# First pairs of the second attention: query evictions on two engines, squares in pieces, another order of products

## The reference

```
q = _rms_norm((hn @ p['w_b_q'][j]).reshape(b, l, B_HEADS, B_HD), p['g_b_qn'][j])   # 16 heads of 64
c_k = jnp.cumsum(logf_all, axis=1)                                                  # forget gates
s = q . k * (d ** -0.5) + (c_q - c_k);  s = where(mask, s, -inf)
p = softmax(s, axis=-1);  o = p . v
h = h + o.reshape(b, l, B_HEADS * B_HD) @ p['w_b_out'][j]
```

## Time and profile before

| | |
|---|---|
| median of 3 runs (lowest to highest) | 2285.42 us (2283.72 to 2291.73) |
| the profiled execution, its own time | 2283.86 us |
| its span, first to last instruction | 2281.5 us |
| mean granted clock of TensorE | 0.987 |
| first scores of pair 0 begin | 1676.78 us from the span's start |
| first transposes of pair 0 / second head's transposes | 1685.74 / 1698.30 us |
| pair 0 ends, pair 1 ends, pair 2 ends | 1714.27 / 1737.24 / 1757.15 us |

### The profile page before, as it was taken

The page is one execution under the profiler, slowest core; times in us unless marked ns, Lnnn a source line. Parts: engine busy times, 40 slices in busy tenths (PEclk is TensorE's granted clock), DMA queues, the critical chain, the costliest instruction groups (busy, mean ns, idle before and its releaser), DMA issues.

```text
span 2281.5 us, 45750 instructions
## 1 busy us (share of the span) xinstructions
PE 2226.9 (98%) x16695; PEld 2147.8 (94%) x16695; DVE 1687.2 (74%) x2718; ACT 1084.9 (48%) x1832; POOL 308.4 (14%) x276
## 2 busy tenths in 40 slices
PE   8999999999999999999999999999989999999998
PEld 8999999988889999999978999999878899999998
DVE  7984984478886896697446995896367868966983
ACT  6542543456765652354324551453257755533541
POOL 0000002035552000000123000001134520000001
PEclk9999999999999999999999999999999999999999
DMA  3222232100002222222223322223212222232222
GB/s 115 92 100 94 93 116 93 46 26 21 15 19 74 84 101 90 89 108 100 73 86 111 112 99 95 93 92 121 74 48 48 50 75 81 95 105 87 93 100 78
DMA packets 73903, 187.58 MB, mean 82 GB/s; under 512 B 40853, under 2 KB 44389, under 8 KB 62537
## 3 DMA queue, kind: packets, MB, share of 16 engines
q1 hardware_dynamic: 72520, 181.73, 23.5%
q0 software_dynamic: 1280, 4.49, 0.6%
HBM read 178.75 MB, written 7.35 MB: 82 GB/s over the span
## 4 chain that ended last, share of the span: by engine, by line
PE 89%; DVE 6%; ACT 2%; issue 2%; DVEq 0%; POOL 0%; DMA 0%; ACTq 0%; SPq 0%
PE ps L731 21%; PE ps L665 19%; PE ps L667 18%; PE ps L666 18%; PE ps L834 6%; PE ps L1104 1%; PE ps L929 1%; PE ps L1040 1%; PE ps L683 1%; DVE hid_lo L2045 1%; PE ps L1131 1%; DVE arena L2499 0%; DVE x_lo L2045 0%; DVE stat L2402 0%; DVE w_lo L2035 0%
## 5 line engine op out<-in xcount | busy, mean ns | idle before, releaser
L665 PE MATMUL ps<-xs_hi,w_hi 128*128 128x272 f32 x1408 | 409.4, 291 | 1.1 <-DVE scratch L2153 1.1
L667 PE MATMUL ps<-xs_hi,w_lo 128*128 128x272 f32 x1408 | 407.9, 290 | 0.0
L666 PE MATMUL ps<-xs_lo,w_hi 128*128 128x272 f32 x1408 | 407.1, 289 | 0.0
L1402 ACT ACTIVATE w_hi<-raw 128x1408 fp32r<-128x1408 f32 (+4 forms) x123 | 146.1, 1188 | 456.8 <-PE ps L731 223.9
L1463 ACT ACTIVATE w_hi<-w_blocks 128x1024 fp32r<-128x1024 f32 x176 | 186.9, 1062 | 308.8 <-PE ps L667 157.8
L666 PE MATMUL ps<-xs_lo,w_hi_more 128*128 128x272 f32 x1056 | 306.6, 290 | 0.0
L665 PE MATMUL ps<-xs_hi,w_hi_more 128*128 128x272 f32 x1056 | 306.5, 290 | 0.0
L665 PEld LDWEIGHTS ps<-xs_hi,w_hi 128*128 128x128 f32 x1408 | 266.2, 189 | 2.3 <-issue 1.3
L731 PE MATMUL ps<-hid_hi,w_hi 128*128 128x256 f32 (+1 forms) x1290 | 265.7, 287 | 1.3 <-DVE w_lo L2035 1.0
L667 PEld LDWEIGHTS ps<-xs_hi,w_lo 128*128 128x128 f32 x1408 | 266.9, 190 | 0.0
L666 PEld LDWEIGHTS ps<-xs_lo,w_hi 128*128 128x128 f32 x1408 | 266.3, 189 | 0.0
(11 more groups left out here) (307 smaller groups left out, 5051.3 us busy)
## 6 DMA issues: line engine op xcount, KB each, us to landing
w_blocks<-w_ffn_in SPq DMA_DIRECT2D x88, 1024.0 KB, 4.8
raw<-w_ffn_out SPq DMA_DIRECT2D x64, 704.0 KB, 4.1
raw<-w_b_kv SPq DMA_DIRECT2D x16, 512.0 KB, 3.2
raw<-w_a_out SPq DMA_DIRECT2D x8, 512.0 KB, 3.3
raw<-w_b_q SPq DMA_DIRECT2D x8, 512.0 KB, 3.3
raw<-w_b_out SPq DMA_DIRECT2D x8, 512.0 KB, 3.3
raw<-w_a_in SPq DMA_DIRECT2D x4, 672.0 KB, 3.9
raw<-w_a_qup SPq DMA_DIRECT2D x8, 288.0 KB, 2.9
```

The costliest lines, as they stand in the source:

```text
L665: pe.matmul(out, lhs[0], rhs[0], start=start, stop=False, skip_group_check=more)
L666: pe.matmul(out, lhs[0], rhs[1], start=False, stop=False, skip_group_check=more)
L667: return pe.matmul(out, lhs[1], rhs[0], start=False, stop=stop, skip_group_check=more)
L1402: act.activation(wh[par][:, 0:n], raw[par][:, 0:n], ACT.Copy).then_inc(w_hi, 1)
```

## The change

1. Taking the second chunk: tiles 0, 1, 2 go to ScalarE (`take_query`), between its first exponentials; tiles 3 and 4 stay with VectorE and come after the reciprocals of the first head. `inverse_sum(0, 4, 0)` moves behind `top(1, 0, 0)`.
2. TensorE no longer waits for c0 and c4 ahead of pair 0. Inside pair 0 it waits for c1, c2 (ScalarE's) and c4 where the banks are first written. Of the 22 `keep_clock` matmuls 4 stay, ahead of `turn(0, 0, 0)`.
3. Squares and sums of the second chunk are made tile by tile: ScalarE squares tile 0, 1, 2, 3 and 4 at four places of pair 0, VectorE sums tiles 0, 1, 2 at three places of pair 0 and tiles 3, 4 at the end of pair 1, where it also makes the means.
4. A tiny exponential (`load_exp`) is issued on ScalarE ahead of `low_rows`.
5. In every staged pair the products `values(0, p)` j = 1, 2, 3 stand together; the wait for the bank of `ts` is ahead of j = 3, not of j = 1, and the transposes `ts` come after all of them.
6. Pair 1 is written out too; the loops cover pairs 2 to 6.

```diff
 TOKQ = {"act": ["sq", "sq4"], "dve": ["c0", "c1", "c2", "c3", "c4", "ss", "ss4", "ms"]}
+TOKQ1 = {"act": ["c0", "c1", "c2"] + [f"sq{t}" for t in range(5)],
+         "dve": ["c3", "c4"] + [f"ss{t}" for t in range(5)] + ["ms"]}
...
     def pair_b(p, stages):
         uses, before = w_uses(L, p, True, stages, False, mla), w_uses(L, p - 1, True, True, stages, mla)
+        first = isinstance(p, int) and p == 0
         scores(1, 0, p)
+        if first:
+            pe.wait_ge(*Q["k"][1]["act"].at("c1"))
+            keep_clock(7, 4, xa[0])
         turn(0, 0, p, uses, before)
+        if first:
+            pe.wait_ge(*Q["k"][1]["act"].at("c2"))
         turn(0, 1, p, uses, before)
         scores(1, 1, p)
+        if first:
+            pe.wait_ge(*Q["k"][1]["dve"].at("c4"))
         turn(0, 2, p, uses, before)
         scores(1, 2, p)
-        if isinstance(p, int) and p == 0:
-            keep_clock(7, 10, xa[0])
         scores(1, 3, p)
...
-        values(0, p, range(1, 2), (lambda: bank_of("ts", uses, before)) if stages else None)
+        values(0, p, range(1, 4), (lambda: bank_of("ts", uses, before)) if stages else None)
         if stages:
             staged_samples(p + 1, uses)
-        values(0, p, range(2, 4))
         if not stages:
             first_tile(XO, range(2))
         turn(1, 0, p, uses, before, not stages)
...
         for u in range(5):
-            if u == 3:
-                pe.wait_ge(*Q["k"][1]["dve"].at("c0"))
-            if u > 2:
-                keep_clock(7, 6, xa[0])
             scores(0, u, 0)
-        pe.wait_ge(*Q["k"][1]["dve"].at("c4"))
         pair_b(0, True)
-        with pe.Fori(1, PAIRS - 1) as p:
+        pair_b(1, True)
+        with pe.Fori(2, PAIRS - 1) as p:
             pair_b(p, True)
         pair_b(PAIRS - 1, False)
...
+def load_exp():
+    act.activation(stat[:, ST_X:ST_X + 1], eps[:, 0:1], ACT.Exp)
...
-    def pair_b(p, first, stages):
+    def pair_b(p, first, stages, squares=None):
         if not first:
             heads_out(p - 1)
+        elif squares is not None:
+            squares(0)
         split_p(0, 0, p)
         split_p(0, 1, p)
         exp(1, 0, p)
...
         exp(1, 1, p)
         exp(1, 2, p)
         stage_values(p)
+        if squares is not None:
+            squares(1)
         split_p(0, 3, p)
         exp(1, 3, p)
         if stages:
...
         exp(1, 4, p)
         if stages:
             stage_samples(p + 1)
-        if first:
-            meanwhile()
         split_p(1, 0, p, not stages)
         split_p(1, 1, p, not stages)
+        if squares is not None:
+            squares(2)
         if stages:
             exp(0, 0, p + 1)
         split_p(1, 2, p, not stages)
...
         if stages:
             exp(0, 3, p + 1)
             exp(0, 4, p + 1)
+        if squares is not None:
+            squares(3)
+            squares(4)
...
-            exp(0, u, 0)
-        pair_b(0, True, True)
-        with act.Fori(1, PAIRS - 1) as p:
+        exp(0, 0, 0)
+        take(0)
+        exp(0, 1, 0)
+        exp(0, 2, 0)
+        take(1)
+        exp(0, 3, 0)
+        take(2)
+        exp(0, 4, 0)
+        pair_b(0, True, True, squares)
+        pair_b(1, False, True)
+        with act.Fori(2, PAIRS - 1) as p:
             pair_b(p, False, True)
         pair_b(PAIRS - 1, False, False)
...
+def take_query(t):
+    if t == 0:
+        act.wait_ge(w_used, Q["u"] + 7 + PRIME + 1)
+    act.activation(qv[1][:, t, :], ps[:, QUERY_BANKS[NT + t], :], ACT.Copy, scale=rtok[:, t:t + 1]
+                   ).then_inc(Q["k"][1]["act"].sem, 1)
+
+def square_query(t):
+    if t < 3:
+        act.wait_ge(*Q["k"][1]["act"].at(f"c{t}"))
+    else:
+        act.wait_ge(*Q["k"][1]["dve"].at(f"c{t}"))
+    if t == 0:
+
+        act.wait_ge(*Q["k"][0]["dve"].at("ss4"))
+    dst = scr[:, t * 512:(t + 1) * 512] if t < 4 else q_sq[:, :]
+    act.activation(dst, qv[1][:, t, :], ACT.Square).then_inc(Q["k"][1]["act"].sem, 1)
+
 def square_queries(c):
-    st, src = Q["k"][c], qn[:, :, 8 * c:8 * c + 8, :].rearrange("p t g w -> p t (g w)")
+    st, src = Q["k"][c], qv[c]
     act.wait_ge(*st["dve"].at("c4"))
-    if c == 1:
-
-        act.wait_ge(*Q["k"][0]["dve"].at("ss4"))
...
+load_exp()
 low_rows(Q, Q["u"] + 7, 1, QUERY_BANKS[2 * NT - 1], 512, Q["k"][0]["dve"].at("c4"))
-attention(X, False, gbq, None, None, lambda: square_queries(1))
+attention(X, False, gbq, None, None, take_query, square_query)
...
-    def pair_b(p, first, stages):
+    def pair_b(p, first, stages, means=(None, None, None)):
         top(1, 0, p)
         if not first:
             heads_out(p - 1)
+        else:
+            inverse_sum(0, 4, p)
         top(1, 1, p)
         top(1, 2, p)
         inverse_sum(1, 0, p)
         split_p(0, 0, p)
         inverse_sum(1, 1, p)
         split_p(0, 1, p)
+        if means[0] is not None:
+            means[0]()
         top(1, 3, p)
         split_p(0, 2, p)
         inverse_sum(1, 2, p)
...
             stage_samples(p + 1)
         inverse_sum(1, 4, p)
         split_p(1, 0, p, not stages)
-        if first:
-            meanwhile()
         if stages:
             top(0, 0, p + 1)
             top(0, 1, p + 1)
...
             inverse_sum(0, 2, p + 1)
             top(0, 4, p + 1)
             inverse_sum(0, 3, p + 1)
+            if means[1] is not None:
+                means[1]()
             inverse_sum(0, 4, p + 1)
+            if means[2] is not None:
+                means[2]()
     if mla:
...
     else:
         top(0, 0, 0)
         top(0, 1, 0)
-        take(0)
-        take(1)
         inverse_sum(0, 0, 0)
         top(0, 2, 0)
-        take(2)
-        take(3)
-        take(4)
         top(0, 3, 0)
         inverse_sum(0, 1, 0)
         inverse_sum(0, 2, 0)
         top(0, 4, 0)
         inverse_sum(0, 3, 0)
-        inverse_sum(0, 4, 0)
-        pair_b(0, True, True)
-        with dve.Fori(1, PAIRS - 1) as p:
+        take(3)
+        take(4)
+        pair_b(0, True, True, means[0:3])
+        pair_b(1, False, True, means[3:6])
+        with dve.Fori(2, PAIRS - 1) as p:
             pair_b(p, False, True)
         pair_b(PAIRS - 1, False, False)
     if part is None:
...
     dve.tensor_scalar(stat[:, ST_QV:ST_QV + NT * HEADS].rearrange("p (t g) -> p t g", t=NT)[:, :, 8 * c:8 * c + 8],
                       stat[:, ST_SS:ST_SS + 40].rearrange("p (t g) -> p t g", t=NT), 1.0 / DB, EPS, ALU.mult,
                       ALU.add).then_inc(inc, 1)
+
+def sum_query(t):
+    st = Q["k"][1]
+    dve.wait_ge(*st["act"].at(f"sq{t}"))
+    src = scr[:, t * 512:(t + 1) * 512] if t < 4 else q_sq[:, :]
+    dve.reduce_sum(stat[:, ST_SS + 8 * t:ST_SS + 8 * t + 8], src.rearrange("p (g w) -> p g w", w=DB), AX.X
+                   ).then_inc(st["dve"].sem, 1)
+
+def mean_query():
+    st = Q["k"][1]
+    dve.wait_ge(*st["dve"].at("ss4"))
+    dve.tensor_scalar(stat[:, ST_QV:ST_QV + NT * HEADS].rearrange("p (t g) -> p t g", t=NT)[:, :, 8:16],
+                      stat[:, ST_SS:ST_SS + 40].rearrange("p (t g) -> p t g", t=NT), 1.0 / DB, EPS, ALU.mult,
+                      ALU.add).then_inc(st["dve"].sem, 1)
+
+def last_means():
+    sum_query(4)
+    mean_query()
 def normalise(st, x):
     dve.wait_ge(*st["pool"].at("pow"))
...
         attention(X, False, gbq, None, ("q0", "q1", "s"))
 def take_second(t):
-    if t == 0:
+    if t == 3:
         dve.wait_ge(w_used, U + 7 + PRIME + 1)
     take_queries(1, t)
-attention(X, False, gbq, None, None, take_second, lambda: mean_square_queries(1))
+attention(X, False, gbq, None, None, take_second,
+          [lambda: sum_query(0), lambda: sum_query(1), lambda: sum_query(2), None, lambda: sum_query(3),
+           last_means])
 out_proj(XO)
 ffn_all(F3)
```

More of the change, by code:

```diff
@@ L79 @@
 ST_F = 216
+ST_X = 40
 ST_N = 296
@@ L367, in build @@
                      wsum=WSUM, wsplit=WSPLIT, hidden=HIDDEN, tokva=TOKVA, att=ATT, out=HEADS_OUT,
-                     stage=STAGE, stageq=STAGEQ, projq=PROJQ, projk=PROJK, first=FIRST, latent=LATENT, tokn=TOKN, tokq=TOKQ, tokv=TOKV, spread=SPREAD,
+                     stage=STAGE, stageq=STAGEQ, projq=PROJQ, projk=PROJK, first=FIRST, latent=LATENT, tokn=TOKN, tokq=TOKQ, tokq1=TOKQ1, tokv=TOKV, spread=SPREAD,
                      samples=SAMPLE, lowrows=LOWROWS, final=FINAL, forget=FORGET, fstage=FSTAGE, resplit=RESPLIT, relow=RELOW, yout=YOUT)
@@ L433, in build @@
                  sst=run("samples"), lows=run("lowrows", 2), paired=2,
-                 k=[run("tokq"), run("tokq")])
+                 k=[run("tokq"), run("tokq1")])
         X = dict(d=DBX, stage=run("stage", PAIRS), stageq=run("stageq", PAIRS), stagev=run("stagev", PAIRS), head0=run("head0x", PAIRS),
@@ L1674, in _, with attention @@
             square_latents("sq", Q_OFF, Q_RANK, ST_MS)
-            def attention(L, mla, g_q, g_k, part=None, meanwhile=None):
+            def load_exp():
+                act.activation(stat[:, ST_X:ST_X + 1], eps[:, 0:1], ACT.Exp)
```

(16 more changed lines are left out.)

## The result

Six runs of the changed kernel have a median of 2272.22 us (2265.63 to 2276.23), six of the kernel before 2284.57 us. The ratio is 0.9939, with a 95% interval of 0.9924 to 0.9954: 12.35 us less where 17.6 were forecast. The profiled execution spans 2271.4 us against 2281.5, at a mean granted clock of 0.985. Both profiles are single executions: the one of before is among its better ones (0.987, where its runs have 0.985 on the mean), the one of the change among its worse (0.985 against 0.9865).

The account below looks back on a forecast made before the run. TensorE, busy 98% of the span, was taken as the bound, so only its idle or low-clock time could be won: 2.6 + 1.4 + 7.5 + 3.6 + 2.5 = 17.6 us less, 2268 us expected, range 2264 to 2277.

Parts of the forecast that it names:

- A: The forecast case for the whole kernel: 17.6 us less, 2268 us, own range 2265 to 2271; chance 0.60.
- a stretch at 0.50: Sign of a wrong prediction: TensorE at granted clock 0.50, that is 1.2 GHz, in pair 0 or 1.
- B: Rival: the clock falls all the same in pairs 0 and 1; only 9.7 us less, 2275.7 us; chance 0.20.
- The head: First scores to T0 (first transposes of pair 0's head 0): earlier table load, fewer useless matmuls; 2.6 us less.
- T0 to T1: Pair 0, first transposes of head 0 to those of head 1: 11.1 us instead of 12.56, 1.4 us less.
- T1 to the end: Pair 0 from head 1's first transposes: squares and sums hide in idle times; 8.45 us instead of 15.97, 7.5 less.
- the order's 0.5: Part 5: products j = 1 and 2 run in TensorE's wait ahead of j = 1; 0.5 us less each staged pair.
- Pair 1: The whole pair: 19.4 us instead of 22.97, 3.6 us less, all of it the tail of the low clock.
- The loop: Pairs 2 to 6: the order of products makes each 0.5 us shorter, 2.5 us less together.
- The stall: Pair 0: TensorE stands 2.74 us before pair 1's fourth score, behind squares and sums; forecast to go, with the low clock.
- Rival C: The pieces (squares, sums, means) do not hide in idle times of VectorE and ScalarE: 2272 us; chance 0.15.
- rival D: Slower: the clock falls early in pair 0 and does not rise in the loop; three such pairs give 2310; chance 0.05.

Follow-up runs that it names:

- e4_block_back: The changed kernel with the five squares on ScalarE, and the sums and means on VectorE, made in a block again: 2283.24 us, ratio 0.9992.
- e9_late_table: The changed kernel without the tiny exponential `load_exp()`, so the table load stands behind the low rows again: 2274.35 us.
- e5_pieces_alone: The kernel before with parts 3 and 6 alone, its head and order of products kept: 2276.27 us, ratio 0.9958.
- e12_all_keeps_again: The changed kernel with 10 useless matmuls in the head and two more ahead of the fourth transposes in every pair: 2263.31 us, ratio 0.9896.
- e10_ten_back: The changed kernel with ten useless matmuls put back ahead of score (1, 3) of pair 0, four in the head: 2270.91 us.
- e11_pair_keeps_alone: The changed kernel, its head with four useless matmuls, plus two ahead of the fourth transposes in every pair: 2266.75 us.

## Why the prediction was right, and which step was not

**The time** lies in the range, the sign is right, and 12.35 us is just beyond the bound of 0.5%, 11.4 us (the interval's end, 0.9954, is not). But the forecast case, A, was not what happened: 2272.22 lies outside A's own range of 2265 to 2271, and a stretch at 0.50 stands in pairs 0 and 1, which the prediction had named as a sign that it is wrong. It was A's instructions with B's clock. That the time was met is owed to the width of the range, which had been drawn to take in B.

**The head: 2.6 forecast, 1.9 measured.** With the clock at 1.00 it is 6.27 us, 2.7 less. The rest is the four matmuls at 1.2 GHz, which I had placed in a wait and which outgrew it.

**T0 to T1: 11.1 forecast, 14.18 measured, 10.50 at full clock.** The loop's own T0 to T1 became 10.07 (1748.23 to 1758.30), so pair 0's differences from the loop (the pieces, the missing heads_out) cost 0.43 there together, where I charged 0.6.

**T1 to the end: 8.45 forecast, 8.95 measured.** Not the pieces: the loop without them now takes 8.77 from T1, since T1 comes 0.95 earlier and the next scores wait 0.3 for the samples' split behind it. I had booked the order's 0.5 in one place, and it is +0.95 and -0.4.

**Pair 1: 19.4 forecast, 22.64 measured, 19.48 at full clock. The loop: 0.5 a pair forecast, 0.56 measured.**

**The step that failed** is the one against rival B: "the head and T0 to T1 held 1.00 with TensorE busy only 6.92 of 8.96 us, and the loop holds 1.00". That was the stream with its 22 useless matmuls in it, twelve of them in the head. I took from it that a head as thin as this one keeps the clock, and then took the useless matmuls out of it. With four or none in the head the clock fell there in seven of seven profiles, with ten or twelve in none of seven. What in the stream decides is not shown: ahead of the fall TensorE was busy 2.70 of 3.40 us, while before it kept the clock through its wait of 1.42 us ahead of T0. B was given 0.20 and priced at 9.7 us less; it happened in the profiles of the change both times, and the measured 12.35 lies between it and A. B's gain was put 2.7 us too low: at equal clock the change is 12 us faster than before, and its mean clock is 0.0015 higher even so. The stall's own low stretch is the likely reason, since e4_block_back, where the stall is back, loses 0.0039 of clock.

The rule of the Trainium skill beside rival B (TensorE: Matmul & The Clock Gate, "A second HAM failure mode: psum-queue depth-cycling") fits what came: the change's profile goes down and up four times between the head and pair 7, with waits of 0.2 to 0.7 us and none above 1 us. It does not say when: the loop of the kernel before has two waits a pair, 0.43 and 0.56 us, and held 1.00 from 1725 us to the end of pair 7. The other place of the Trainium skill (ScalarE: Activation LUTs, "What ACT_TABLE_LOAD costs") adds a drain that this trace does not show: the load takes 1.28 us, and without the early load the head of e9_late_table is 1.29 us longer, not 2.66.

**Rival C** is refuted by e5_pieces_alone (T0 to T1 12.61 us with the pieces, 12.56 without) and e12_all_keeps_again, **rival D** by the time and by the loop, which returned to 1.00 in every profile.

Open: what decides whether the fall in the head lasts 13.6 us (the change, twice) or 3.4 us (e4_block_back, e10_ten_back, e11_pair_keeps_alone) under the same TensorE code. It began 4.2 us behind the first scores in the two long cases and 4.4 us behind them in the three short ones, and no run varied that alone. Open too: what the clock did in the change's fastest run (2265.63 us at a mean clock of 0.990), which has no profile; and which of the pair's waits matters, as only one place was filled.

## What to carry to other kernels

A matmul whose result nobody reads can be worth its time: before it is removed, ask what the clock will do with the thinner stream, and put it where the engine waits anyway (two ahead of each pair's fourth transposes cost the pair nothing, and the mean was 5.7 us lower, with a standard error of 1.8). Where runs scatter, list each run's time against its mean clock: the 3.8 us of the order of products, which the medians hid, came out at equal clock. And before a low stretch that got shorter is put down to added instructions, look whether they ran before it ended; here they had not. A block of side work on two engines can be spread without cost if each piece is set against an idle time read from the loop's timeline.

## What the runs showed of the hardware

A low stretch is not always paid for by a long wait: ahead of the fall in the head TensorE was busy 2.70 of 3.40 us at 0.99. Nor is one needed at all: in the kernel before TensorE was busy for the whole 3.40 us ahead of a low stretch of 3.4 us that begins at 759.3 us. A busy TensorE does not end it soon either: 13.6 us in the change, with TensorE busy 13.50 of them. How long it lasts is not fixed by TensorE's code: 13.6 us in both profiles of the change, 3.4 us in e4_block_back with the same code, and in e10_ten_back and e11_pair_keeps_alone, whose code is the change's up to the rise. Two executions of one kernel can repeat each other to about 0.02 us in each stretch from the head to pair 2, low clock and all, while others of it differ by 10 us.
